# Rows of activations 256 elements apart instead of 260, and two buffers of moving operands that begin 48 bytes later

## The reference

```python
h = h + 0.5 * swiglu(rmsnorm(h, ffn1_norm[i]), ffn1_w_gu[i], ffn1_w_down[i])
u = rmsnorm(h, mix_norm[i])
b_g, c_g, v_c, q_c, kv_c, k_r, g_conv, g_mla = jnp.split(u @ w_in[i], split_pts, axis=-1)
...
m = jnp.square(jax.nn.relu(jnp.einsum('bsd,df->bsf', m, w_up[i])))
m = jnp.einsum('bsf,fd->bsd', m, w_down[i])
```

## Time and profile before

| | |
|---|---|
| runs | 2272.36 us median of 3 (2271.99 to 2274.2) |
| profiled execution | 2272.34 us, its span 2270.5 us |
| mean granted clock of TensorE | 0.926 |
| TensorE matmul (PE) | 1980.6 us busy, 87% |
| TensorE weight load (PEld) | 1949.0 us, 86% |
| VectorE (DVE) | 1463.4 us, 64% |
| ScalarE (ACT) | 1016.6 us, 45% |
| GpSimd (POOL) | 204.1 us, 9% |

### The profile page before, as it was taken

The page is one execution under the profiler, slowest core; times in us unless marked ns, Lnnn a source line. Parts: engine busy times, 40 slices in busy tenths (PEclk is TensorE's granted clock), DMA queues, the critical chain, the costliest instruction groups (busy, mean ns, idle before and its releaser), DMA issues.

```text
span 2270.5 us, 40515 instructions
## 1 busy us (share of the span) xinstructions
PE 1980.6 (87%) x15810; PEld 1949.0 (86%) x15810; DVE 1463.4 (64%) x1713; ACT 1016.6 (45%) x1221; POOL 204.1 (9%) x168
## 2 busy tenths in 40 slices
PE   5999999899979999998999958657999587479996
PEld 5999999899979999998999958547999576479996
DVE  5556777665565556777555657875555678846556
ACT  4434355543445444455444445544333455433333
POOL 2000000000001000000000023501000135010000
PEclk8999999999989999999999978768999887679998
DMA  5555354455544555444555523112555331125551
GB/s 193 185 185 185 121 171 157 133 189 186 187 147 148 185 185 158 137 157 149 167 185 185 174 93 98 56 56 86 191 186 170 120 112 61 41 90 169 187 180 60
DMA packets 254428, 330.67 MB, mean 146 GB/s; under 512 B 6342, under 2 KB 228484, under 8 KB 254276
## 3 DMA queue, kind: packets, MB, share of 16 engines
q1 hardware_dynamic: 253748, 327.47, 44.2%
q10 hardware_dynamic: 432, 0.92, 0.1%
q0 software_dynamic: 96, 0.26, 0.1%
HBM read 327.58 MB, written 1.05 MB: 145 GB/s over the span
## 4 chain that ended last, share of the span: by engine, by line
issue 48%; PE 36%; DVE 8%; POOL 4%; ACT 3%; DVEq 0%; POOLq 0%; ACTq 0%
PE work L1727 9%; PE work L1728 8%; PE work L1729 8%; PE acc L1727 3%; PE acc L1729 3%; PE acc L1728 3%; POOL fa L639 2%; DVE fa L1524 2%; POOL fa L667 1%; ACT w_hi L710 1%; ACT fa L953 1%; DVE w_lo L1119 1%; DVE fa L1160 0%; DVE fa L1495 0%; DVE xl L1149 0%
## 5 line engine op out<-in xcount | busy, mean ns | idle before, releaser
L1727 PE MATMUL work<-xh,w_hi 128*128 128x256 f32 x3184 | 921.5, 289 | 97.3 <-DVE xl L1149 63.9
L1119 DVE TENSOR_TENSOR w_lo<-raw,w_hi 128x2048 fp32r<-128x2048 f32 (+1 forms) x318 | 707.6, 2225 | 413.0 <-ACT w_hi L710 410.1
L1728 PE MATMUL work<-xl,w_hi 128*128 128x256 f32 x3184 | 912.6, 287 | 0.0
L1729 PE MATMUL work<-xh,w_lo 128*128 128x256 f32 x3184 | 909.1, 286 | 0.0
L710 ACT ACTIVATE w_hi<-raw 128x2048 fp32r<-128x2048 f32 (+1 forms) x318 | 588.2, 1851 | 706.6 <-PE work L1729 451.6
L1727 PEld LDWEIGHTS work<-xh,w_hi 128*128 128x128 f32 x3184 | 620.3, 195 | 109.1 <-DVE xl L1149 70.4
L1728 PEld LDWEIGHTS work<-xl,w_hi 128*128 128x128 f32 x3184 | 622.4, 195 | 0.6
L1729 PEld LDWEIGHTS work<-xh,w_lo 128*128 128x128 f32 x3184 | 620.9, 195 | 0.0
L1727 PE MATMUL acc<-ra,w_hi 128*128 128x256 f32 x1344 | 377.9, 281 | 6.3 <-DVE ra L1678 3.3
L1729 PE MATMUL acc<-ra,w_lo 128*128 128x256 f32 x1344 | 377.4, 281 | 0.0
L1728 PE MATMUL acc<-ra,w_hi 128*128 128x256 f32 x1344 | 377.3, 281 | 0.0
(11 more groups left out here) (236 smaller groups left out, 1886.7 us busy)
## 6 DMA issues: line engine op xcount, KB each, us to landing
raw<-in_ffn_w_gu_dram SPq DMA_DIRECT2D x88, 1024.0 KB, 5.1
raw<-in_w_in_dram SPq DMA_DIRECT2D x56, 1024.0 KB, 5.4
raw<-in_ffn_w_down_dram SPq DMA_DIRECT2D x44, 1024.0 KB, 5.0
raw<-in_w_up_dram SPq DMA_DIRECT2D x32, 1024.0 KB, 5.4
raw<-in_w_down_dram SPq DMA_DIRECT2D x32, 1024.0 KB, 5.0
raw<-in_w_mla_out_dram SPq DMA_DIRECT2D x8, 1024.0 KB, 5.2
raw<-in_w_o_dram SPq DMA_DIRECT2D x8, 1024.0 KB, 5.5
raw<-in_w_ple_gate_dram SPq DMA_DIRECT2D x8, 1024.0 KB, 5.2
```

Of the source, the lines that this page charges most:

```text
L1119: v.tensor_tensor(w_lo[:, s, 0:n], raw[:, s, 0:n], w_hi[:, s, 0:n].bitcast(F32), ALU.subtract).then_inc(lo_done.sem, 1)
L1727: pe.matmul(dst, ah, bh, start=start and i == 0, stop=False, skip_group_check=not group)
L1728: pe.matmul(dst, ah, bl, start=False, stop=False, skip_group_check=not group)
L1729: last = pe.matmul(dst, al, bh, start=False, stop=stop and i == len(pairs) - 1, skip_group_check=not group)
```

## The change

The rows of xh, xl, hh and hl become 256 elements apart, like all others. xh and xl become two cuts of one tensor `xa` whose first 12 elements (48 bytes) are left unused, and the arena ra gets 12 unused elements ahead of it. No instruction is added or removed.

```diff
-ROW = T + 4
+
+XPAD, RPAD = 12, 12
...
-        xh = sb("xh", [P, KD, ROW], F32R)[:, :, 0:T]
-        xl = sb("xl", [P, KD, ROW], F32R)[:, :, 0:T]
+        xa = sb("xa", [P, XPAD + 2 * KD * T], F32R)[:, XPAD:]
...
-        ra = sb("ra", [P, 10240], F32R)
+        ra = sb("ra", [P, RPAD + 10240], F32R)[:, RPAD:]
...
+        xh, xl = (cut(xa, i * KD * T, KD, T) for i in range(2))
         gs, si, us, hid = (cut(fa, i * 1024, 2, 2, T) for i in range(4))
-        hh, hl = (cut(ra, i * 4 * ROW, 2, 2, ROW)[:, :, :, 0:T] for i in range(2))
+        hh, hl = (cut(ra, i * 4 * T, 2, 2, T) for i in range(2))
```

## The result

The kernel after takes 2286.24 us (median of 5 runs, 2283.95 to 2288.01), the kernel before 2272.36: a ratio of 1.0056, 95% interval 1.0042 to 1.0071. The forecast of 2264 us had the wrong sign, and the result lies just above the range that ended at 2284. The profiled execution took 2283.95 us with a span of 2282.1, against 2272.34 and 2270.5 before.

The account below looks back on a forecast made before the run. The prediction took TensorE's matmul start distance as the bound in four stretches; -11.7 us for xh and xl and +3.3 for ra gave -8.4, from 2272.34 to 2264 us. The 8-in-10 range was 2236 to 2284 us.

Parts of the forecast that it names:

- What bounds the kernel: In four stretches, 1545 of 2270.5 us, TensorE's distance from one matmul's start to the next sets the end.
- Matmuls that read xh and xl: In the four stretches, 7306 matmuls go from 117.4 to 115.8 ns at constant offset 48: -11.7 us.
- rival A: Stagger was worth something: the row step sets the distance, constant offsets cost 118.3 ns; 2279 to 2284 us, chance 0.25.
- The measure of 64 bytes: Row places in SBUF counted from multiples of 64 bytes, putting xh and xl at 48 and ra at 16.
- Matmuls that read ra: 5136 matmuls, nearly all in the four stretches, go from some 118.35 to 119.0 ns at offset 16: +3.3 us.
- The other stretches: Outside the four stretches, 2246 matmuls read xh and xl; counted as 0, at most -3.6 us.
- B: Rival: xh/xl and ra effects cancel, or nothing matters because the stationary side sets the distance; about 2272 us, chance 0.15.
- C: Rival: offsets 48 and 16 are both good, xh/xl and ra matmuls all at 115.0 ns; 2238 us, chance 0.20.

Follow-up runs that it names:

- e2: Against the kernel before: rows still 260 elements apart, but xh and xl step by 16 from 48 bytes and ra is at 80; 2282.62 us, ratio 1.0034.
- e8: Against the kernel after: pads of 28 and 24 elements, so xh and xl at 112 bytes and ra at 64 within 128; 2241.81 us, ratio 0.9852.
- e4: Against the kernel after: xh and xl put back as before, only ra changed, at 16 bytes within 128; 2259.28 us, ratio 0.9934.
- e7: Against e4: ra another 64 bytes later, at 80 within 128; 2275.94 us, ratio 1.0004.
- p4: Probe of matmuls alone: activations and weights each moved from 0 to 112 bytes by 16, 64 combinations; 113.3 to 123.4 ns a matmul.
- p3: Probe of matmuls alone in the kernel's order: x and ra each moved from 0 to 112 bytes by 16; x at 96 took 120.0 ns, at 112 113.7.
- e1: Against the kernel after: both pads 0, so equal rows with xh and xl at 0 and ra at 96; 2296.51 us, ratio 1.0097.
- e5: Against the kernel after: xh moved to 16 bytes, xl at 48, ra at 80; 2284.42 us, ratio 1.0039.
- e10: Against the kernel after: pads of 48 and 8 elements, xh, xl and ra at 192 past the weights' start within 256 bytes; 2241.94 us, ratio 0.9856.
- p2: Probe of matmuls alone: pairs of constant xh and xl offsets, each run after a wait and after stepping rows; (0, 32) took 120.0 and 116.9 ns.
- p1: Probe of matmuls alone: one layout of moving rows and weights per line; rows all at 0 took 120.0 ns, at 48 118.3.

## Why the prediction was wrong

**What bounds the kernel: right.** The effect went through the distance of TensorE's starts in the stretches of the earlier trace rows, nothing through the engines beside it: VectorE is busy 1463.0 us (1463.4 before), ScalarE 1015.7 (1016.6). The 213 ns at the lower level stayed.

**Matmuls that read xh and xl: the step that failed.** I had taken 115.8 ns for a constant offset of 48, for -11.7 us. Measured: 118.35, and 8900 x (118.35 - 117.52) = +7.4 us. Two thirds of the weight in 115.8 came from rows 3 and 7 of one block, as if a row's time were the price of its offset. The block was no accident: over 142 such blocks of that trace row 3 takes 116.4 ns a matmul, row 7 115.0, the six others 117.8 to 118.8. But the reading was wrong twice. Row 7 is at 48 only within 64 bytes; within 128 it is at 112. And a row within a changing sequence shows that sequence, not the price of its offset: the row at 48 takes 116.4 ns in the kernel before, 117.0 in e2, and 118.35 where all rows are at 48; the row at 112 takes 115.0, 117.3, and 113.4 where all are at 112 (e8, once settled). The long constant run of the earlier trace rows pointed the right way, and it was the one that spoke for rival A.

**The measure of 64 bytes: wrong, and it hid the gain.** The prediction named it a choice that no row shows. e4 and e7 differ by exactly 64 bytes and by 0.7%; p4 against p3 says that 128 matters too, and so does e4 beside p3's stepping rows with ra at 16, 128 bytes off (114.22 against 118.6 ns).

**Matmuls that read ra: the sign right, the size near.** Predicted +3.3 us. Measured A 4024 x 0.33 = +1.3 and R 954 x 0.91 = +0.9 us. That this is near is luck, since the place was wrong: the change puts ra at 80 within 128, and e4, which has it at 16, is faster.

**The other stretches, taken at 0.** They hold some 1900 of the 8900 matmuls of X, 1.6 us of its term. Not foreseen at all were the 50 more matmuls at the lower level, +4.7 us, which shorter waits (-4.0) nearly cancel.

**The rivals.** A had the right sign and a fair size (2279 to 2284, measured 2286) at a chance of 0.25. Its number, a constant offset at 118.3, was what X did, but by luck: it came from ra at 96, and constant places in p3 lie between 113.3 and 120.0. Its reason, that the stagger itself is worth something, is only half of it: the constant 0 of e1 is indeed worse than the stagger, but the stagger of e2 is worse than that of before, and the constant 112 of e8 is better than the stagger of before by 3.4 ns. B failed: both terms were losses, nothing cancelled. Its other ground, a distance set by the stationary side alone, fell too: e1 and e8 have the weights at the same place, and X is 119.82 and 114.17 ns. C said that both places are good at 115 ns, for 2238 us. The places were not, but the pace it put its price on exists, and e8 comes to 2242 us. Of the rules weighed there, the Trainium skill's "Advanced Engine Details and Errata", section SBUF Cachelines, has lines of 16 bytes in SBUF. That starts at multiples of 16 are therefore all alike, as I had worked out from it, does not hold for this pace: among such starts p4 has 113.3 to 123.4 ns.

**What stays open.** What in the memory or the engine makes the pace depend on both places; why some distances of p4 don't follow their diagonal; what decides whether a run enters a fast pace or a slow one (115.5 or 118 ns in e5, 113.3 or 118 in e10); and why e8 runs 143 more matmuls at the lower clock level. No experiment separates these.

## What to carry to other kernels

Where one matmul follows another with a new weight load each time, try the place of the moving operand against the place of the weights over at least 256 bytes before any theory of it: between the worst and the best placement tried lie 2.4% (2296.51 and 2241.81 us), with not one instruction changed. When a tensor's size or padding changes, look where every later tensor lands, since 64 bytes of it alone gave or took 15.5 us here (e4, e7). And take the price of a placement from a long steady run of it, never from single rows of a sequence that mixes placements.

## What was unexpected of the hardware

- Some values of the pace come back again and again: of p4's 64 combinations 20 show 120.0 ns, 9 show 118.7 and 7 show 113.3. Within a run it is steady: e8's projection keeps to 113.3 ns once its first dozen is through.
- It has a memory: p2's 120.0 and 116.9, e10's 113.3 and 117.8, and the 120.0 and 118.3 of the kernel after are the same code at the same addresses.
- Rows 4 bytes off a multiple of 16 gave 123.3 ns (L77), but so did one of p4's combinations in which all starts are multiples of 16 (123.4).
- 128 columns cost 111.7 ns a matmul, hardly less than 256, and 512 cost 226.7, from the starts of p1's L85 and L86. So the moving columns don't set the distance at 128; with a load of 128 columns of weights for each matmul, the stationary side probably does, though no run took the loads away. The Trainium skill's "TensorE: Matmul & The Clock Gate", section LDWEIGHTS, has such a load cost its columns over 1.2 GHz, an estimate of 106.7 ns; the measured 111.7 is 5 ns above. The same page's "Step-by-step: what each phase is for" says that loading the next weights takes no read bandwidth from the running matmul; p1's 120.0 against 118.35 ns, with only the weights moved by 16 bytes, shows that the place of the weights changes the running pace all the same. Whether read bandwidth is the reason no run shows.
